# Recurrence inputs of a hybrid decoder block as token-stationary products, and the scans of the value product in other places

## The reference

```python
h = xn @ w_in                                        # 256 x 2048 times 2048 x 6144
q, k, v, g, u, y = jnp.split(h, [R, 2*R, 3*R, 4*R, 4*R + L], axis=-1)   # R = L = 1024
uc = causal_dwconv(u, conv_w, conv_b)                # 4 taps along the tokens
# rg_lru, in 8 blocks of 128 channels
r = sigmoid(ub @ w_a + b_a); i = sigmoid(ub @ w_x + b_x)
log_a = 8 * r * log_sigmoid(lam);  a = exp(log_a)
b = sqrt(-expm1(2 * log_a)) * (i * uc)
h_t = a_t * h_(t-1) + b_t                            # scan over 256 tokens
lru = h * gelu(y)
```

## Time and profile before

| | |
|---|---|
| median of 3 runs | 1484.94 us (1484.76 to 1485.3) |
| profiled execution: its own time, its span | 1484.75 us, 1483.0 us |
| PE busy | 1473.9 us, 99% of the span |
| DVE busy, ACT busy | 1023.5 us (69%), 1001.9 us (68%) |
| the chain that ended last | PE 99% |
| HBM read | 286.19 MB, 194 GB/s over the span |

### The profile page before, as it was taken

One profiled execution on the slowest core, in us unless ns is written; L12 is line 12 of the kernel. 1 busy time (PEld: TensorE's weight loads), 2 busy tenths in 40 slices (PEclk: granted clock), 3 DMA queues, 4 the chain that ended last, 5 costly groups with the idle time before them and its releaser, 6 DMA issues.

```text
span 1483.0 us, 21458 instructions
## 1 busy us (share of the span) xinstructions
PE 1473.9 (99%) x6926; PEld 1235.4 (83%) x6926; DVE 1023.5 (69%) x1369; ACT 1001.9 (68%) x1545; POOL 2.9 (0%) x9
## 2 busy tenths in 40 slices
PE   9999999999999999999999999999999999999997
PEld 8888888888888888888888888888888888888886
DVE  6755566788887567675565777675867667585696
ACT  6647878854555487564868868586766858676974
POOL 0000000000000000000000000000000000000000
PEclk9999999999999999999999999999999999999999
DMA  9766655565556555445555565656555555655554
GB/s 345 262 204 213 209 189 186 196 207 171 171 170 230 195 185 189 152 157 172 196 186 191 191 198 187 196 184 198 186 198 198 193 188 190 200 188 193 192 198 142
DMA packets 81045, 289.01 MB, mean 195 GB/s; under 512 B 9009, under 2 KB 10545, under 8 KB 80097
## 3 DMA queue, kind: packets, MB, share of 16 engines
q1 hardware_dynamic: 76752, 275.68, 55.9%
q10 hardware_dynamic: 3744, 9.30, 1.8%
q0 software_dynamic: 496, 3.34, 0.6%
HBM read 286.19 MB, written 2.10 MB: 194 GB/s over the span
## 4 chain that ended last, share of the span: by engine, by line
PE 99%; ACT 0%; DVE 0%; ACTq 0%; issue 0%; POOL 0%; POOLq 0%
PE ps L295 99%; PE ps L356 0%; PE ps L497 0%; PE ps L447 0%; ACT scr L991 0%; ACT vm L1006 0%; DVE xres L1537 0%; ACTq L118 0%; POOL ones L281 0%; ACT sm_ L1002 0%; DVE rcol L1544 0%; DVE sm_ L1540 0%; DVE sm_ L1541 0%; POOLq L1652 0%
## 5 line engine op out<-in xcount | busy, mean ns | idle before, releaser
L1016 DVE TENSOR_TENSOR wlo<-raw,whi 128x1024 fp32r<-128x1024 f32 x516 | 625.1, 1220 | 339.6 <-ACT whi L588 324.1
L588 ACT ACTIVATE whi<-raw 128x1024 fp32r<-128x1024 f32 x516 | 532.6, 1054 | 239.1 <-PE ps L295 230.0
L295 PE MATMUL ps<-whi,xT 128*128 128x512 f32 x1792 | 556.1, 390 | 0.0
L295 PE MATMUL ps<-whi,mixT 128*128 128x512 f32 x1728 | 535.4, 390 | 0.0
L295 PEld LDWEIGHTS ps<-whi,xT 128*128 128x128 f32 x1792 | 336.4, 188 | 69.7
L295 PEld LDWEIGHTS ps<-whi,mixT 128*128 128x128 f32 x1728 | 324.6, 188 | 67.9 <-issue 0.3
L295 PE MATMUL ps<-wlo,xT 128*128 128x512 f32 x896 | 348.7, 389 | 0.0
L295 PE MATMUL ps<-wlo,mixT 128*128 128x512 f32 x864 | 334.9, 389 | 0.0
L295 PE MATMUL ps<-xT,whi 128*128 128x512 f32 x640 | 222.9, 399 | 0.0
L295 PEld LDWEIGHTS ps<-wlo,xT 128*128 128x128 f32 x896 | 168.2, 188 | 34.6
L295 PEld LDWEIGHTS ps<-wlo,mixT 128*128 128x128 f32 x864 | 162.2, 188 | 33.4
(11 more groups left out here) (187 smaller groups left out, 665.7 us busy)
## 6 DMA issues: line engine op xcount, KB each, us to landing
raw<-in_stream SPq DMA_DIRECT2D x518, 512.0 KB, 3.3
xres<-in_xin ACTq DMA_DIRECT2D x2, 1024.0 KB, 7.8
scr<-in_xt_in ACTq DMA_DIRECT2D x8, 256.0 KB, 4.6
xres<-in_xin POOLq DMA_DIRECT2D x1, 2048.0 KB, 12.2
out_x<-vm SPq DMA_DIRECT2D x8, 256.0 KB, 3.1
raw<-in_stream SPq DMA_DIRECT2D x4, 256.0 KB, 4.3
kT<-in_memt_in ACTq DMA_DIRECT2D x2, 512.0 KB, 6.2
vbuf<-in_memin ACTq DMA_DIRECT2D x1, 1024.0 KB, 10.4
```

Source lines behind the costliest of these rows:

```text
L295: return nc.tensor.matmul(o, l, r, start=start, stop=stop, skip_group_check=True)
L588: A(whi[:, 2 * pr + s, :], raw[:, 2 * pr + s, :], ACT.Copy).then_inc(hi_done, 1)
L1016: V.tensor_tensor(wlo[:, 2 * pr + s, :], raw[:, 2 * pr + s, :], f32(whi[:, 2 * pr + s, :]), ALU.subtract).then_inc(lo_done, 1)
```

## The change

The 16 chunks of `u` and `y` become wide: four windows of four chunks, one window for 512 channels (`u`, `u`, `y`, `y`), results with tokens on the partitions. ACT scales each into `yu_rows` (two operations of 128 x 512), DVE turns it in 32 x 32 blocks (two transposes), and the blocks are moved to their places by 16 copies of 32 x 256, 8 on ACT and 8 on DVE. Taps, gates, tanh and the multiplication by the input gate (`gated`) are written out block by block in the slots of 16 steps and the first two of the value product; gelu is done twice, over 1024 elements. The gate weights are loaded by two DMAs of POOL early in the kernel instead of eight of ACT in the loop. The move of the last keys stands in the first four of the 16 steps. In the value product coefficient, scan and split of one block now stand in one step (steps 3, 4, 5 and 6/7).

```diff
-            narrow(C_YU // 2, 0, xT, {KT - 2: lambda: wait_for(xt_lo, KT)})
-            narrow(C_YU // 2, 1, xT)
-            with pe.Fori(1, LB) as n:
-                narrow(C_YU // 2 + n, 0, xT, {6: lambda: [gates_of(n), 3][1]})
-                narrow(C_YU // 2 + n, 1, xT)
+            for n in range(16):
+                if n < 4:
+                    pe.wait_ge(xt_lo, 4 * n + 4)
+                wide(C_YU // 2 + n // 2, n % 2, xT, range(n % 4 * 4, n % 4 * 4 + 4), (4, 0, 2, 4)[n // 4], n % 4 == 0, n % 4 == 3,
+                     (lambda: gates_of(n - 9)) if n >= 9 else None)
```

POOL's loads of the gate weights:

```diff
+            pool.wait_ge(lo_done, 16)
+            for i, b in enumerate((dmask, scrg)):
+                pool.dma_start(b[:], gates[4 * i:4 * i + 4].rearrange("n p c -> p n c")).then_inc(gw_in, 16)
```

ACT in the 16 steps of the recurrence inputs (`move_yu` is four copies, `first_taps` four operations, `recur` three tanh):

```diff
+            between = {0: lambda: move_keys(3, 0), 1: lambda: move_keys(3, 2), 2: lambda: move_keys(3, 3),
+                       3: lambda: keep_yu(0), 4: lambda: move_yu(0, 1), 5: lambda: first_taps(0),
+                       7: lambda: keep_yu(1), 8: lambda: move_yu(1, 1), 9: lambda: first_taps(1), 10: lambda: recur(1),
+                       11: lambda: keep_yu(2), 12: lambda: move_yu(2, 0), 13: lambda: move_yu(2, 1),
+                       15: lambda: keep_yu(3)}
+            behind = {0: lambda: move_keys(3, 1), 3: lambda: move_yu(0, 0), 7: lambda: move_yu(1, 0), 9: lambda: recur(0),
+                      12: lambda: recur(3), 13: lambda: recur(4), 14: lambda: recur(5), 15: lambda: recur(6)}
```

ACT in the value product:

```diff
+            between = {0: lambda: recur(7), 1: lambda: move_yu(3, 1), 2: lambda: gelus(1)}
+            behind = {0: lambda: move_yu(3, 0), 1: lambda: (ch.wait(), gelus(0)), 2: lambda: lru_root(0),
+                      3: lambda: (lru_part(0), lru_root(1)), 4: lambda: (lru_part(1), lru_root(2)),
+                      5: lambda: (lru_part(2), lru_root(3)), 6: lambda: lru_part(3)}
```

DVE in the 16 steps (`turn_yu` is two transposes, `move_yu` four copies, `taps` three operations):

```diff
+            between = {3: lambda: turn_yu(0), 4: lambda: move_yu(0, 3), 6: lambda: taps(1), 7: lambda: turn_yu(1),
+                       8: lambda: move_yu(1, 3), 10: lambda: taps(5), 11: lambda: turn_yu(2), 12: lambda: move_yu(2, 3),
+                       13: lambda: taps(7), 14: lambda: gated(4), 15: lambda: turn_yu(3)}
+            behind = {3: lambda: move_yu(0, 2), 5: lambda: taps(0), 6: lambda: taps(2), 7: lambda: move_yu(1, 2),
+                      8: lambda: taps(3), 9: lambda: taps(4), 10: lambda: gated(0), 11: lambda: move_yu(2, 2),
+                      12: lambda: (taps(6), gated(2)), 13: lambda: gated(3), 15: lambda: move_yu(3, 2)}
+            before = {11: lambda: gated(1), 15: lambda: gated(5)}
```

DVE in the value product, whose scans stood in pairs of steps before:

```diff
+            before = {0: lambda: gated(6), 1: lambda: gated(7), 3: lambda: lru_coef(0), 4: lambda: lru_coef(1), 5: lambda: lru_coef(2),
+                      6: lambda: v_out(0), 7: lambda: v_out(1)}
+            between = {0: lambda: move_yu(3, 3), 3: lambda: lru_scan(0), 4: lambda: lru_scan(1), 5: lambda: lru_scan(2),
+                       6: lambda: (lru_coef(3), lru_scan(3))}
+            behind = {3: lambda: lru_split(0), 4: lambda: lru_split(1), 5: lambda: lru_split(2), 7: lambda: lru_split(3)}
             for n in range(8):
-                do0 = (lambda: v_out(n - 6)) if n >= 6 else None
-                if n % 2:
-                    step(C_V // 2 + n // 2, 1, do0, lambda: lru_scan(n // 2), lambda: lru_split(n // 2))
-                else:
-                    step(C_V // 2 + n // 2, 0, do0, lambda: lru_coef(n // 2))
+                step(C_V // 2 + n // 2, n % 2, before.get(n), between.get(n), behind.get(n))
```

More of the change, by code:

```diff
@@ L63 @@
 NC = C_F + 2 * NF + NF
-W_YU, W_H, W_Q = 0, 16, 40
+W_H = 0
 PAN = 1024
@@ L233, in q_move, with yu_move, gate_weights, gate_bank @@
                     q_blocks[i * 32:(i + 1) * 32, q])
+        def yu_move(w, i, q):
+            half, dst = 4 * (w % 2), (uT, gel)[w // 2]
+            return (dst[q * 32:(q + 1) * 32, half:half + 4, :].rearrange("p j (t i b) -> p j t i b", t=TT, i=4)[:, :, :, i, :],
+                    yu_blocks[i * 32:(i + 1) * 32, q])
+        def gate_weights(k):
+            return (dmask, scrg)[k // 4][:, k % 4, :]
+        def gate_bank(k):
+            return (bankA, bankB)[k % 2]
+        def tanhs(k):
+            return scr[:, 4 + 2 * (k % 2), :], scr[:, 5 + 2 * (k % 2), :]
         def mem_tile(f):
@@ L727, in _ @@
                 step(C_KM // 2 + n // 2, n % 2, before_split, between, behind)
-            act.wait_ge(halves_set, 1)
[L730 to L755, removed]
@@ L756, in _, with keep_yu, move_yu, moved @@
-            ch.leave(LB)
-            act.dma_start(dmask[:], decay).then_inc(mask_in, 16)
+            def keep_yu(w):
+                for tt in range(TT):
+                    A(yu_rows[:, tt, :], ps[:, (4, 0, 2, 4)[w] + tt, :], ACT.Copy, scale=rcol[:, 1, tt:tt + 1]).then_inc(yu_kept, 1)
+            def move_yu(w, i):
+                act.wait_ge(yu_turned, 2 * w + 2)
+                for q in range(4):
+                    A(*yu_move(w, i, q), ACT.Copy).then_inc(yu_moved_act, 1)
+            def moved(w):
+                act.wait_ge(yu_moved_act, 8 * w + 8)
+                act.wait_ge(yu_moved_dve, 8 * w + 8)
@@ new lines, in first_taps, with recur @@
+            def first_taps(half):
+                moved(half)
+                for n in range(4 * half, 4 * half + 4):
+                    A(lru_gx[:, n, :], uT[:, n, :], ACT.Identity, scale=par[:, 4 * n + (O_CW + 3):4 * n + (O_CW + 4)],
+                      bias=par[:, n + O_CB:n + O_CB + 1]).then_inc(uc0_done, 1)
+            def recur(k):
+                act.wait_ge(gates_done, k + 1)
+                if k > 1:
+                    act.wait_ge(gx_done, k - 1)
+                o, (tr, ti) = gate_bank(k), tanhs(k)
+                ch.link(A(tr, o[:, :T], ACT.Tanh, scale=0.5, bias=halves[:, k:k + 1]))
+                A(ti, o[:, T:], ACT.Tanh, scale=0.5, bias=halves[:, k + LB:k + LB + 1]).then_inc(i_ready, 1)
+                ch.mark(A(lru_t[:, k, :], tr, ACT.Tanh, scale=cs[:, k:k + 1], bias=cs[:, k:k + 1]))
@@ new lines, in gelus @@
+            def gelus(half):
+                moved(2 + half)
+                y = gel[:, 4 * half:4 * half + 4, :]
+                A(y, y, ACT.Gelu_apprx_tanh)
+            act.wait_ge(halves_set, 1)
+            between = {0: lambda: move_keys(3, 0), 1: lambda: move_keys(3, 2), 2: lambda: move_keys(3, 3),
[3 more added lines that the diff above has]
+                       15: lambda: keep_yu(3)}
@@ L761, in lru_root @@
+            behind = {0: lambda: move_keys(3, 1), 3: lambda: move_yu(0, 0), 7: lambda: move_yu(1, 0), 9: lambda: recur(0),
+                      12: lambda: recur(3), 13: lambda: recur(4), 14: lambda: recur(5), 15: lambda: recur(6)}
+            for n in range(16):
+                step(C_YU // 2 + n // 2, n % 2, (lambda: recur(2)) if n == 11 else None, between.get(n), behind.get(n))
             def lru_root(n):
@@ L769, in lru_part @@
                 A(mixT[:, LB + n, 0, :], tmp[:, 5, :], ACT.Copy).then_inc(lru_hi, 1)
-            ch.wait()
+            between = {0: lambda: recur(7), 1: lambda: move_yu(3, 1), 2: lambda: gelus(1)}
+            behind = {0: lambda: move_yu(3, 0), 1: lambda: (ch.wait(), gelus(0)), 2: lambda: lru_root(0),
+                      3: lambda: (lru_part(0), lru_root(1)), 4: lambda: (lru_part(1), lru_root(2)),
+                      5: lambda: (lru_part(2), lru_root(3)), 6: lambda: lru_part(3)}
             for n in range(8):
-                keys = (lambda: move_keys(3, n)) if n < 4 else None
-                if n % 2:
-                    step(C_V // 2 + n // 2, 1, None, keys, lambda: lru_part(n // 2))
-                else:
-                    step(C_V // 2 + n // 2, 0, None, lambda: lru_root(n // 2), keys)
+                step(C_V // 2 + n // 2, n % 2, None, between.get(n), behind.get(n))
             def silus(h1):
@@ L1183, in _ @@
             cos_sin()
[L1186 to L1217, removed]
@@ L1218, in _, with turn_yu, move_yu @@
-            ch.leave(LB)
+            def turn_yu(w):
+                dve.wait_ge(yu_kept, 2 * w + 2)
+                if w:
+                    dve.wait_ge(yu_moved_act, 8 * w)
+                for tt in range(TT):
+                    V.transpose(yu_blocks.rearrange("p q j t b -> p t j q b")[:, tt], yu_rows[:, tt, :]).then_inc(yu_turned, 1)
+            def move_yu(w, i):
+                dve.wait_ge(yu_turned, 2 * w + 2)
+                for q in range(4):
+                    V.tensor_copy(*yu_move(w, i, q)).then_inc(yu_moved_dve, 1)
@@ new lines, in taps @@
+            def taps(n):
+                dve.wait_ge(uc0_done, n + 1)
+                for tap in (2, 1, 0):
+                    sh = 3 - tap
+                    ins = V.scalar_tensor_tensor(out=lru_gx[:, n, sh:], in0=uT[:, n, :T - sh],
+                                                 scalar=par[:, 4 * n + (O_CW + tap):4 * n + (O_CW + tap + 1)],
+                                                 in1=lru_gx[:, n, sh:], op0=ALU.mult, op1=ALU.add)
```

(17 more changed lines are left out.)

38 lines of the change are left out of this document (21 added, 17 removed).

## The result

The changed kernel takes 1490.44 us (median of 7 runs, 1488.79 to 1491.98) against 1484.76 (7 runs, 1484.64 to 1485.3): a ratio of 1.0036, 95% interval 1.0025 to 1.0048. It is slower, by 5.7 us. The forecast was slower by 3.2 us (1488.1), range 1482.9 to 1491.2. Not only the median moved: these 7 runs of the kernel before lie within 0.7 us of each other, those of the changed one within 3.2.

What follows compares the result with a forecast made beforehand. PE was taken to bound the kernel (99% of the chain). PE's gain of 1.98 us and the value product's loss of 5.2 gave +3.2, so 1487.95 us, with 0.2 for the median 1488.1; range 1482.9 to 1491.2.

Steps and rivals of the forecast that it cites:

- PE's part: Recurrence inputs: 16 narrow chunks with 7 gate pairs, 95.28 us, become wide ones at 93.3 us, a gain of 1.98.
- No stall in the 16 steps: Recurrence inputs: added ACT and DVE work fits behind PE's chunks of 5.44 us (6.33 with a gate pair), costing nothing.
- The value product: Value product into H0: DVE steps 3, 4 and 5 take 7.04 us each against PE's 5.44, a loss of 5.2 us.
- The 0.3 us between the last split and PE: Middle of H0: estimated time from the second panel being ready until PE multiplies, 0.3 us within the 5.2 us loss.
- The long gelus: ACT in steps 1 and 2 of the value product: two gelus over 1024 elements, 1.05 us each, bounds 0.42 to 1.7.
- the drain: ACT's table switches in steps 1 and 2: some 1380 ns more each by the skill, which would make the loss 6.7 us.
- the sum of 3.2: Whole kernel: PE's gain of 1.98 us against the value product's loss of 5.2 us, +3.2 us, slower by 0.22%.
- rival A: H0: the clock falls to half in the stall, another 2.8 us for half of H0, 1490.9 us; chance 0.17.
- signs of being wrong: PE idle through ACT, a DMA near 50 us, or not at all; clock below 1 behind 310 us; wide chunk not 5.44.
- the ledger: Value product and H0: DVE's panels against due times step by step; H0's second panel ready at 29.44 us, stall some 2.9.
- Rival C: Near PE's chunk 8: early gate loads collide with 95% busy DMA, adding 0.5 to 3.1 us, 1489 to 1491; chance 0.08.

Runs made afterwards that it cites:

- the fastest kernel: The changed kernel with coefficients and scans of the value product spread over more steps and gate weights loaded late: 1482.90 us, ratio to before 0.9987.
- two kernels that differ in nothing else: The changed kernel with scans spread, gate weights loaded early (1483.67 us) or late (1482.90 us).
- the kernels with this stretch: Kernels with H0's idle stretch unfilled: the changed kernel (1490.44 us), it with gate weights late (1489.74), and the kernel before with packing alone (1491.69).
- the packed kernel before: The kernel before with only the places of coefficient, scan and split in the value product changed to those of the changed kernel: 1491.69 us, ratio 1.0046.

## Why the prediction was right, and where it was short

**PE's part: right.** 1.98 us was said, 1.89 measured in the windows; a gate pair costs 0.91 us in these wide chunks (a chunk with one takes 6.35), not 0.89, and there are seven. In the fastest kernel all of it arrives in the median (2.0 us). By the rule of the Trainium skill that was weighed there (TensorE: Matmul & The Clock Gate, Back-to-back issue gap) the gain was an estimated 0.3 us. The Trainium skill gives that formula, in the same section, for a single matmul by itself; here a weight load stands ahead of every matmul. The trace does not agree with it: a wide chunk of 24 matmuls takes 5.44 us and not 5.18, in every trace here.

**No stall in the 16 steps: right.** The window is 93.38 or 93.39 us in all seven traces of this form, and PE is busy in all of it.

**The value product: right in mechanism, place and size, and shown by taking the packing out and by putting it alone into the kernel before.** 5.2 us was the term; the stall without a fall of the clock measures 5.06. The 0.3 us between the last split and PE was too much: 0.05 in the trace. The long gelus took 1.05 us each (1.05 was taken), and a table load of 1.28 us is followed by the next operation in 0.01 us (0.02 in the earlier trace rows):

```profile
290.24 1.28 ACT L784 ACT_TABLE_LOAD   x1
291.53 1.06 ACT L784 ACTIVATE gel<-gel 128x1024 f32<-128x1024 f32 x1
```

So the drain of which the Trainium skill tells (ScalarE: Activation LUTs, What ACT_TABLE_LOAD costs) cost nothing here.

**What the sum of 3.2 left out.** The measured median is 2.3 us above the forecast and outside the forecast's own range, 1487.0 to 1489.5; it lies in the stated one, 1482.9 to 1491.2, because that took in rival A. Two of the signs of being wrong that the prediction named were there: a granted clock below 1 behind 310 us, and a wait of PE that goes back to a DMA near 50 us. The failing step is the choice of the likeliest case, with the clock and the early load at nothing: both things that were set beside it as rivals came on top of it.
- Rival A (chance 0.17) happened in at least 3 of 7 runs by their clock, one of them the profiled run, which is also the median. Its price was put at 2.8 us for half of H0; it is 1.6, and 2.0 in the execution profiled first, where H1 to H4 also ran 0.1 us longer each. The evidence in hand was read too lightly: the stall that the ledger gave, 2.9 us, was longer than the idle 2.4 us after which the clock fell in the earlier trace rows. That A's own figure, 1490.9, is within 0.5 us of the measured one is partly luck: what it put too high for the fall, the late panels and the slower H1 to H4 (0.55 and 0.42) made up.
- Rival C (0.08) happened in part. 1.05 MB in a stretch with the DMA engines 95% busy was costed at nothing because ACT had waited there at most 0.7 us. It is 0.65 us in the profiled run and 0.8 in the median between two kernels that differ in nothing else. The cover was read from one execution: with the early load, chunks 10 and 11 are late in the traces of two kernels of four, and in none of the five traces without it. The loads start at 43.47 us, with PE at the end of chunk 6, and not at chunk 8 as the prediction has it; its sum does not hang on that.

So 1484.8 - 1.9 + 5.06 + 0.55 = 1488.5 us is the changed kernel in a run without a fall (its lowest was 1488.79), and 1490.1 and more with one. A fall in H0 was forecast as the less likely case; in the kernels with this stretch it is at least an even one (8 or more of 16 runs), and the median fell on its side.

What stays open: in which of two executions with the same idle stretch the clock falls, and why; and why a panel's landing near 50 us varies so much between executions (a trace with late loads has ACT waiting 9.0 us for panels there, and no chunk late), and with it how often the early load costs and how much.

## What to carry to other kernels

When steps hold an engine that is only 69% busy, the average says nothing: add up each step against the pace of the engine that bounds the kernel, and carry the lateness from step to step until it meets its due time. Of three steps of 7.04 us in a row against 5.44, the second and the third exceed the pace by 3.2 us together; less the 1.2 us by which the first was early that leaves 2.0, and 2.2 was measured. Spreading coefficients and scans over emptier steps returned the 5 us of the stall in both stages, and no run with them spread shows a fall. A stall of PE has a second price, the clock, so a stall as long as one after which the trace shows the clock falling must be counted with it, and it can be bought off with idle matmuls if the stall itself can't be removed. A load of a megabyte that nobody waits for should start where DMA has room, not at the first moment at which its buffer is free; here that was worth 0.8 us in the median.

## What the runs showed of the hardware

- The same idle stretch of PE (2.5 us in the record) ends at a clock of 1.00 in one execution and at 0.50 in another of the same form; runs of the changed kernel alone stand at 0.997 and at 0.999, so it is the execution that differs, not the kernel. In the changed kernel the fall came 0.26 us after PE had resumed, in the packed kernel before 0.90 us after; it lasted 3.41 us in both.
- The start of the kernel has such a spread too. The clock rises at 4.28, 5.83, 6.25 or 9.89 us in different executions, and chunk 0 takes 5.54 to 7.48 us. Between the traces of the two kernels with scans spread it is all that differs: chunk 1 begins at 11.92 us in one and at 13.23 in the other, 1.3 us apart, and the spans (1481.8 and 1483.0) are 1.2 apart.
- Narrow chunks have two paces, 5.547 and 5.65 us. Which one H1 to H4 have does not depend on the fall alone: after the fall in the changed kernel they took 5.65, after the one in the packed kernel before 5.547. The kernel before has both paces without any fall there: 5.547 from 320 to 345 us, 5.65 from 365 to 385.
